# Attention stage: a key or query job that stands first in its step goes ahead of the step's scores on PE, ahead of its sigmoids on ScalarE and ahead of its scan on VectorE

## The reference

```
proj = rms_norm(x) @ w_in                       # a | gate | q | k | v
c = silu(layer_norm(causal_conv(a * sigmoid(gate))))
q, k = rms_norm(q), rms_norm(k)                 # per head, 8 heads of 64
z = q @ k^T * 64**-0.5                          # blocks of 128 queries
log_keep = where(valid, log_sigmoid(-z), 0)
later = reverse_cumsum(log_keep) - log_keep
o = where(valid, exp(log_sigmoid(z) + later), 0) @ v
x = x + concat(c, rms_norm(o)) @ w_out
x = x + top2_of_32_experts(rms_norm(x))
```

## Time and profile before

| | |
|---|---|
| median of 3 runs | 2157.6 us (2156.3 to 2159.7) |
| profiled execution | 2158.2 us, of which the span of its instructions is 2156.5 us |
| PE busy | 2078.7 us, 96% of the span |
| DVE, ACT, POOL busy | 1602.6, 1258.3, 768.8 us |
| attention, 506 to 1251 us | 745 us of the span |

### The profile page before, as it was taken

One profiled execution on the slowest core, in us unless ns is written; L12 is line 12 of the kernel. 1 busy time (PEld: TensorE's weight loads), 2 busy tenths in 40 slices (PEclk: granted clock), 3 DMA queues, 4 the chain that ended last, 5 costly groups with the idle time before them and its releaser, 6 DMA issues. The chain is left out here.

```text
span 2156.5 us, 40174 instructions
## 1 busy us (share of the span) xinstructions
PE 2078.7 (96%) x13523; PEld 1754.6 (81%) x13524; DVE 1602.6 (74%) x2056; ACT 1258.3 (58%) x2199; POOL 768.8 (36%) x697
## 2 busy tenths in 40 slices
PE   8999999998899999899999979999999999999998
PEld 6888888886787887688888767888888888888887
DVE  3799999997676667867878868698698466466644
ACT  5322433337677777867767646687687465456643
POOL 1111445564566555645545453122122111111211
PEclk9999999998999999999999999999999999999999
DMA  7564334336433242423232119999899878677851
GB/s 227 179 206 157 119 125 151 118 117 180 121 101 111 84 135 84 119 77 113 72 116 84 55 72 333 357 328 366 299 373 372 268 233 278 198 223 262 285 161 34
DMA packets 211949, 393.18 MB, mean 182 GB/s; under 512 B 54925, under 2 KB 81933, under 8 KB 211821
## 3 DMA queue, kind: packets, MB, share of 16 engines
q1 hardware_dynamic: 198285, 357.42, 48.0%
q0 software_dynamic: 13536, 34.12, 6.8%
HBM read 315.42 MB, written 91.23 MB: 189 GB/s over the span
## 5 line engine op out<-in xcount | busy, mean ns | idle before, releaser
L2663 DVE TENSOR_TENSOR p_w_lo<-p_raw,p_w_hi 128x1024 fp32r<-128x1024 f32 (+1 forms) x196 | 330.5, 1721 | 134.3 <-ACT p_w_hi L2455 134.2
L2253 POOL TENSOR_TENSOR late<-late,p_past 128x1024 f32<-128x1024 f32 (+4 forms) x166 | 308.6, 1860 | 321.5 <-DVE p_past L2097 321.2
L819 DVE SCALAR_TENSOR_TENSOR p_ut<-p_ut,p_cw 128x512 f32<-128x512 f32 (+1 forms) x480 | 329.3, 764 | 0.0
L2455 ACT ACTIVATE p_w_hi<-p_raw 128x2048 fp32r<-128x2048 f32 (+1 forms) x150 | 271.6, 1842 | 62.1 <-PE p_up L2547 53.3
L2097 DVE TENSOR_TENSOR_SCAN p_past<-p_keep,p_past,p_one 128x513 f32<-128x513 f32 (+1 forms) x196 | 225.9, 1193 | 77.4 <-ACT p_keep L1897 76.0
L1897 ACT ACTIVATE p_keep<-p_zp 128x512 f32<-128x512 f32 (+3 forms) x326 | 158.6, 546 | 105.3 <-PE p_zp L1764 94.2
L2547 PE MATMUL p_gp<-p_w_hi,p_xt_hi 128*128 128x256 f32 x736 | 214.3, 291 | 0.0
L490 PE MATMUL p_pj<-p_w_hi,p_xt_hi 128*128 128x512 f32 x512 | 205.7, 402 | 4.2 <-DVE p_xt_lo L795 2.4
L2547 PE MATMUL p_gp<-p_w_lo,p_xt_hi 128*128 128x256 f32 x736 | 206.4, 280 | 0.0
L2547 PE MATMUL p_gp<-p_w_hi,p_xt_lo 128*128 128x256 f32 x736 | 206.4, 280 | 0.0
L490 PE MATMUL p_pj<-p_w_hi,p_xt_lo 128*128 128x512 f32 x512 | 201.0, 393 | 0.0
(11 more groups left out here) (318 smaller groups left out, 4973.9 us busy)
## 6 DMA issues: line engine op xcount, KB each, us to landing
p_raw<-in_w_up SPq DMA_DIRECT2D x96, 512.0 KB
p_raw<-in_w_gate SPq DMA_DIRECT2D x96, 512.0 KB
p_raw<-in_w_down SPq DMA_DIRECT2D x96, 512.0 KB
late<-in_w_up SPq DMA_DIRECT2D x32, 512.0 KB
late<-in_w_gate SPq DMA_DIRECT2D x32, 512.0 KB
late<-in_w_down SPq DMA_DIRECT2D x32, 512.0 KB
wide_raw<-in_w_in SPq DMA_DIRECT2D x56, 256.0 KB, 3.9
wide_raw<-in_x SPq DMA_DIRECT2D x17, 512.0 KB, 5.0
```

What stands on the lines that cost most here:

```text
L819: dve.scalar_tensor_tensor(dst, src, cw[:, a, j:j + 1], dst, ALU.mult, ALU.add).then_inc(tap_done, 1)
L2253: pool.tensor_tensor(mine, mine, past_rows[:, u % NP, 0:n, 2:2 + w], ALU.mult).then_inc(a_done, 1)
L2455: act.activation(part(w_hi, p, wide), ring(n, wide), ACT.Copy).then_inc(whi_done, wide)
L2663: dve.tensor_tensor(part(w_lo, p, wide), ring(n, wide), part(w_hi, p, wide).bitcast(F32), ALU.subtract).then_inc(wlo_done, wide)
```

## The change

A table of the planner becomes the constant `RAMP`. A new function `turned(s)` gives the first job of step s where it is a `k` or a `q` and s is 6 or more. `ahead` leaves that job out, and the three engine loops do it at the head of the step, just before `scores(s)`, `sigmoids(s)` and `scan(s)`. Of the 259 jobs, 38 are moved in this way (21 `k`, 17 `q`). The order of the jobs among themselves, and so their banks, stays the same. No instruction is added or dropped, and the orders of POOL and of SP's DMAs stay the same.

```
+RAMP = [[("k", 0, 1), ("q", 1)], [("k", 0, 2)], [("wo", 0, 0), ("q", 2)], [("k", 0, 3)], [("q", 3), ("wo", 0, 1)],
+        [("k", 0, 4), ("k", 0, PT)]]
...
+        def turned(s):
+
+            return [j for j in jobs[s][0:1] if j[0] in ("k", "q") and s >= len(RAMP)]
+
         def ahead(s):
 
-            return [j for j in jobs[s][0:1] if j[0] != "o"]
+            return [j for j in jobs[s][0:1] if j[0] != "o" and j not in turned(s)]
...
-        order = jobs[-1] + [job for s in range(steps) for job in ahead(s) + behind(s)]
+        order = jobs[-1] + [job for s in range(steps) for job in turned(s) + ahead(s) + behind(s)]
...
             for s in range(steps):
+                for j in turned(s):
+                    job(j)
                 if s < len(units):
                     scores(s)
...
                     split(m)
+                for j in turned(s):
+                    job(j)
                 if s < len(units):
                     sigmoids(s)
...
                     piece(n)
+                for j in turned(s):
+                    job(j)
                 if s < len(units):
                     scan(s)
```

More of the change, by code:

```diff
@@ L1198, in attention_jobs @@
     placed, where, s = {-1: [("k", 0, 0), ("q", 0)]}, {}, 0
-    ramp = [[("k", 0, 1), ("q", 1)], [("k", 0, 2)], [("wo", 0, 0), ("q", 2)], [("k", 0, 3)], [("q", 3), ("wo", 0, 1)],
-            [("k", 0, 4), ("k", 0, PT)]]
+    ramp = RAMP
     waiting = [x for x in waiting if not any(x[3] in js for js in ramp)]
```

## The result

The changed kernel takes 2168.0 us (median of 5 runs, 2163.0 to 2169.7), against 2157.6 us before. The ratio is 1.0043, with a 95% interval of 1.0029 to 1.0058. It is slower, by 9.3 us by the ratio and by 10.4 by the medians. The forecast was 2160.3 us and its range ended at 2166.5.

The account below looks back on a forecast made before the run. PE, busy 96% of the 2156.5 us span, was taken to bound the kernel. Gains of -3.7 and costs of +6.4 us gave net +2.7 on the 2157.6 us median: 2160.3 us, range 2153.5 to 2166.5.

Parts of the forecast that it names:

- Step 9: In step 9, wo(1,0) no longer waits for k21, -1.9 us; half-clock stretch at 551.8 us may go, -0.8.
- the second term: Half-clock stretch from 551.8 to 555.2 us may go as waits shrink: half of 1.7 us taken, -0.8.
- Step 7: In step 7, k5's 1.55 us wait for k18 only moves, making o1 wait longer: 0.
- the prediction's sign: In the profile after, o1 starts near 545 us with a wait of 3 us instead of 1.8.
- Small waits behind moved jobs: Elsewhere, small waits of `wo` behind moved key or query jobs shrink: -1.0 us.
- Late sigmoids: Sigmoids start later behind moved jobs' copies: +0.8 in steps 81 to 84, +0.5 at 81, 86, 88, +0.5 over the rest.
- The dense stretch: Around steps 90 to 96, moved jobs wait bare before the scores: +3.7 us net, bounds 0 and +6.
- step 90's 2.3: In step 90, q22's bare wait adds 1.6 us and o18's wait for k20 0.7: 2.3 by step 91's end.
- Step 139: In step 139, q31 waits bare for k13, about +0.9 us over its former 1.29 us wait.
- a rival of 15%: Bare pauses over about 2 us in steps 88 to 96 bring half-clock stretches, up to 1.7 us each: 2166 us, 15%.
- The prediction's own signs: Wrong if steps 86 to 98 take no longer, o1's wait does not grow, or half-clock stretches change in number.
- Its sign for late sigmoids: In the profile after, PE's waits for sigmoids rise from 5.1 to 7 or 8 us.

Follow-up runs that it names:

- e4: The kernel before with only q22 (step 90) moved: 2161.8 us against 2157.5 for the kernel before, ratio 1.0020.
- e8: The kernel before with only k21 (step 9) and the key job of step 118 moved: 2152.3 us against 2154.5 before, ratio 0.9987.
- e10: The changed kernel with useless matmuls filling the bare waits of steps 90, 92, 94, 96 and 139: 2162.1 us against 2155.2 before, ratio 1.0043.
- e1: The kernel before with only k18 (step 7) and k21 (step 9) moved: 2158.2 us against 2157.5 before, ratio 0.9998.
- e9: The changed kernel run once more, unaltered: 2165.1 us against 2155.2 for the kernel before, ratio 1.0047.
- e3: The kernel before with only the jobs of steps 90, 92, 94, 96 and 139 moved: 2163.5 us against 2157.5 before, ratio 1.0028.
- e5: The changed kernel with nine useless matmuls in the bare wait of step 90 alone: 2163.2 us against 2154.5 before, ratio 1.0039.
- e2: The changed kernel without moving the jobs of steps 90, 92, 94, 96 and 139: 2158.8 us against 2157.5 before, ratio 1.0004.

## Why the prediction was wrong, by its own steps

**Step 9, predicted -1.9 and -0.8 for the clock.** Together -2.7 forecast, 2.5 won. wo(1,0) no longer waits, as said. The half clock did not go, it came 5 us earlier, so the second term's reason was wrong. That the sum held is in part luck: e4 won 1.6 us by step 9 with no job moved there, by a half clock that came 5 us earlier too.

**Step 7, predicted 0.** Right. o1 started at 545.4 us as before, with a wait of 1.97 us for 1.77 and 0.44 and 0.25 us of new waits ahead of it, where the prediction's sign had one wait of 3 us. That ACT sets q5's eviction is its reading of the rows; no run tried it.

**Small waits behind moved jobs, predicted -1.0.** Shown at step 119: e8 goes from -2.4 to -3.2 between steps 97 and 138. The tables show no other gain that lasts.

**Late sigmoids, predicted +0.8 +0.5 +0.5.** Steps 10 to 80 cost 1.3 and 81 to 89 cost 1.9, 3.2 in all against 1.8. The place was wrong too: steps 82 to 84, the largest of the three terms, cost nothing (-1.2 at step 80 and at step 85), and the 1.9 lie in steps 86 to 89. Of the 1.9 a part hangs on where the half-clock stretch near 880 us falls: e10 lost 0.9 there, and e1 0.6 with no job moved. Steps 16 and 20, behind q7 and k8, took 0.6 and 0.5; there ACT had at most 0.1 us of pause before the sigmoids, and PE's scores wait 0.61 and 0.50 us for them that they did not wait before.

**The dense stretch, predicted +3.7 at the full clock.** The mechanism was right and so was its size where the clock stayed up: step 90's 2.3 measured 2.4 (e4) and 2.5 (e10), the bare wait 2.6 measured 2.57, and the stretch to step 97 was 4.0 in e10. Step 139, +0.9, gave 0.0 at the full clock: what it lost came back within two steps.

**The step that failed** is the clock's place in the sum: the sentence that let the dense stretch stand at the full clock, with "one or two such stretches" of half clock as a rival of 15%, because "only one place is so long". In the changed kernel there are half-clock stretches of 6.7, 3.3 and 3.3 us at steps 90, 96 and 139, worth 2.6 us (steps 90 to 97) and 1.4 us by e9 less e10, and one of 6.7 us at 1228, worth 1.8 us (157 to 169, where e10 loses nothing). That makes 5.8 of the 10.3 us that attention lost. It is a figure of attention in these traces; the timed runs of e9 and e10 differ by 2.9 us in the median, within their scatter. Without them the changed kernel would stand 4.5 us above before on this profile, nearer the 2.7 of the sum. The rival's own condition, "idle for over about 2 us at a time", was met at step 90 and at 139, and I had both waits in my hands: 2.6 us, and 1.29 + 0.9 = 2.2 us. The prediction's own signs tell the same: it called itself wrong if the half-clock stretches change in number, and PE's busy time, to stay within 2 us, rose by 7.8. Its sign for late sigmoids, waits up from 5.1 to 7 or 8 us, failed as well (5.3).

The Trainium skill, "TensorE: Matmul & The Clock Gate", section "What's actually happening", has the full clock as something that activity has to hold up. e10 agrees from 885 to 1150 us, with the waits filled and the clock at 1.00, and in all five executions by the granted clock; e3 and e5 show that an unfilled wait need not let it fall. Weighing it only by one row at 1.00 whose waits were 1 us and less, and the earlier trace rows, was the error.

**Open.** Step 158 has the same wait of 2.5 us in every kernel. Behind it the half clock lasts 6.8 us in the changed kernel, e9 and e5, 3.4 us in e10 (at 1222 us), e1, e3 and e8, and does not come in the kernel before, e2 and e4. Why was not tried, nor why e4 kept its clock behind a 2.5 us wait and e3 behind 1.55 and 2.20. The half clock is not settled by one wait's length. So the 1.8 us at 1228 us may not belong to the change at all.

## What to carry to other kernels

A job that goes ahead of the main work must find its input and its buffer ready at the *new* place; the test is to lay the end of the previous holder's eviction against the end of the instruction that now stands before it, job by job, and to move only those that pass. A wait that lay under other work is not only its own length when it is laid bare: on TensorE, give the half clock for the work behind it a price and a chance of its own (here 1.1 to 1.5 us at each of three places, when it came). And where several engines pass a job on, their orders must change together: each half of this change alone cost twice as much as the whole.

## What the runs showed of the hardware that I had not expected

Useless matmuls in a wait cost nothing that shows: with 27 of them, about 6 us of PE work, 265 us stood at clock 1.00 instead of 0.97, the granted clock of the whole was higher in each of five executions (0.988 to 0.989 against 0.985 to 0.987), and from step 89 to step 141 e10 lost 4.0 us where e9 lost 8.0. A gain in the timed runs is not clear of noise.

The same work can get a different clock. Both traces of the changed kernel have their half-clock stretches at the same places within 1 us (880, 890, 918, 1136 and 1228 us). They are also alike in the part that all kernels share: 3.4 us at half clock from 23.6 us on, then 6.8 us from 508 us on. e10, the same code there, has none at 23.6 us and 10.2 us from 505 us on. And e4 differs from before by 1.6 us at step 9 for no reason in its code. A single trace prices a change of 1 or 2 us only if the clock fell at the same places in both.
